# Local attention's maxima in items of two heads and one bank, with a third bank for its scores and a third for its outputs

## The reference, cut to what matters

```python
SWA_WINDOW = 128; SWA_KV_HEADS = 4; SWA_GROUP = 4   # four heads share one key/value head

def _banded_gqa(q, k, v, window, sinks):            # per block of 128 queries
    s = jnp.einsum('bqgrd,bkgd->bgrqk', qblk, kb).astype(jnp.float32) * scale
    s = jnp.where(mask, s, NEG_INF)                 # own block and the one before it
    snk = jnp.broadcast_to(sinks...)
    pr = jax.nn.softmax(jnp.concatenate([s, snk], -1), axis=-1)[..., :-1]
    return jnp.einsum('bgrqk,bkgd->bqgrd', pr, vb)

o * jax.nn.silu(z)
```

## Time and profile before

| | us |
|---|---|
| median of 3 runs | 3054.64 (3053.04 to 3061.67) |
| the profiled execution | 3053.61 |
| its span, first to last instruction | 3051.8 |
| TensorE busy in the span | 2892.7 (95%) |
| VectorE, ScalarE, GpSimd busy | 1938.8, 1590.5, 1392.0 |
| local attention, from the first maxima's product to the last output product | 476.1 to 728.7 |

### The profile page before, as it was taken

One profiled execution on the slowest core, in us unless ns is written; L12 is line 12 of the kernel. 1 busy time (PEld: TensorE's weight loads), 2 busy tenths in 40 slices (PEclk: granted clock), 3 DMA queues, 4 the chain that ended last, 5 costly groups with the idle time before them and its releaser, 6 DMA issues. The chain is left out here.

```text
span 3051.8 us, 41224 instructions
## 1 busy us (share of the span) xinstructions
PE 2892.7 (95%) x13411; PEld 2328.4 (76%) x13411; DVE 1938.8 (64%) x3398; ACT 1590.5 (52%) x2808; POOL 1392.0 (46%) x1139
## 2 busy tenths in 40 slices
PE   8999996888999999999998799999999999899998
PEld 6888884566888788777877588888888878688776
DVE  4543315663578864555664588888888887357875
ACT  3111114666445544444544277777777777534643
POOL 0022104665232540001440388888888889423353
PEclk9999997999999999999999699999999999999999
DMA  5343437565997675455799634435335342498674
GB/s 165 84 136 125 117 118 242 179 203 172 308 277 239 201 247 183 159 177 167 251 328 380 148 73 102 103 73 116 91 78 127 73 92 87 157 301 270 212 243 145
DMA packets 284760, 530.13 MB, mean 174 GB/s; under 512 B 29200, under 2 KB 110992, under 8 KB 277392
## 3 DMA queue, kind: packets, MB, share of 16 engines
q1 hardware_dynamic: 218528, 391.22, 43.3%
q10 hardware_dynamic: 66032, 136.48, 14.7%
HBM read 346.85 MB, written 180.49 MB: 173 GB/s over the span
## 5 line engine op out<-in xcount | busy, mean ns | idle before, releaser
L2609 POOL TENSOR_TENSOR mla_pl<-mla_p,mla_ph 128x512 fp32r<-128x512 f32 (+3 forms) x640 | 702.9, 1121 | 144.4 <-ACT mla_p L2458 141.5
L1523 PE MATMUL end_bank<-end_xh,end_whi 128*128 128x512 f32 x1808 | 718.1, 397 | 44.3 <-DVE end_wlo L1754 17.0
L1525 PE MATMUL end_bank<-end_xh,end_wlo 128*128 128x512 f32 x1808 | 708.2, 392 | 0.0
L1524 PE MATMUL end_bank<-end_xl,end_whi 128*128 128x512 f32 x1808 | 707.6, 391 | 0.0
L1592 ACT CAST end_whi<-early_wraw 128x1024 fp32r<-128x1024 f32 (+1 forms) x204 | 211.4, 1036 | 531.8 <-PE end_bank L1525 510.7
L2457 ACT ACTIVATE mla_ph<-mla_score 128x512 fp32r<-128x512 f32 (+3 forms) x640 | 342.4, 535 | 238.0 <-PE mla_score L2285 232.9
L1754 DVE TENSOR_TENSOR end_wlo<-early_wraw,end_whi 128x1024 fp32r<-128x1024 f32 x188 | 255.4, 1358 | 317.9 <-ACT end_whi L1592 317.7
L1523 PEld LDWEIGHTS end_bank<-end_xh,end_whi 128*128 128x128 f32 x1808 | 342.1, 189 | 134.9 <-DVE end_wlo L1754 24.6
L2542 DVE TENSOR_TENSOR mla_acc<-mla_acc,mla_p 128x512 f32<-128x512 f32 (+3 forms) x576 | 351.0, 609 | 106.6 <-ACT mla_p L2458 104.2
L1524 PEld LDWEIGHTS end_bank<-end_xl,end_whi 128*128 128x128 f32 x1808 | 342.3, 189 | 72.6 <-issue 2.9
L1525 PEld LDWEIGHTS end_bank<-end_xh,end_wlo 128*128 128x128 f32 x1808 | 341.6, 189 | 72.4
(11 more groups left out here) (242 smaller groups left out, 4985.7 us busy)
## 6 DMA issues: line engine op xcount, KB each, us to landing
early_wraw<-in_pe_gate ACTq DMA_DIRECT2D x64, 512.0 KB, 4.9
early_wraw<-in_w_out ACTq DMA_DIRECT2D x62, 512.0 KB, 7.3
early_wraw<-in_w_in ACTq DMA_DIRECT2D x56, 512.0 KB, 3.8
scratch_q<-in_rope SPq DMA_DIRECT2D x64, 256.0 KB, 2.9
swa_q<-scratch_q SPq DMA_DIRECT2D x8, 2048.0 KB, 9.2
end_factor<-scratch_inv SPq DMA_DIRECT2D x64, 256.0 KB, 9.6
scratch_proj<-end_out_f SPq DMA_DIRECT2D x64, 256.0 KB, 6.9
scratch_sum<-end_out_f SPq DMA_DIRECT2D x64, 256.0 KB, 6.3
```

The costliest lines, as they stand in the source:

```text
L1523: nc.tensor.matmul(bank, wh[:, at], xh[:, k0 + k * nq, :], start=(k == 0), stop=False)
L1524: nc.tensor.matmul(bank, wh[:, at], xl[:, k0 + k * nq, :], start=False, stop=False)
L1525: last = nc.tensor.matmul(bank, wl[:, at], xh[:, k0 + k * nq, :], start=False, stop=(k == kc - 1))
L2609: pool.tensor_tensor(p_lo[b][:, off:TC], prob[b][:, off:TC], p_hi[b][:, off:TC].bitcast(F32), ALU.subtract).then_inc(p_lo_ok, 1)
```

## The change

The item of the maxima is cut in two: two heads, 512 columns, one bank. The two `mx` tiles shrink from two banks to one each. The two banks that this frees go to a third score bank (`nscore` 3) and a third output bank (`n_o` 3). A unit has 16 items instead of 8; `share` puts them at 2, 2, 1, 2, 2, 2, 1, 2, 2 in slots 0 to 8 of an even unit and 3, 1, 2, 2, 1, 2, 2, 1, 2 in those of an odd one. An item still waits for the item two before it. The number of products and of DVE instructions is the same, and the maxima land in the same columns. `mla` keeps its banks; only the way its output column is written in the code changes.

```diff
-        lag, nbuf, nscore = (3, 6, 3) if long else (2, 5, 2)
+        lag, nbuf, n_o = (3, 6, 2) if long else (2, 5, 3)
+        nscore = 3
...
-        o_ps = [s.ps(f"o{b}", [P, TC]) for b in range(2)]
+        o_ps = [s.ps(f"o{b}", [P, TC]) for b in range(n_o)]
...
                 pe.wait_ge(probs, g + 1)
-                if st["first"] and c >= 2:
-                    pe.wait_ge(row_ok, c - 1)
+                if st["first"] and c >= n_o:
+                    pe.wait_ge(row_ok, c - n_o + 1)
                     if not long:
-                        pe.wait_ge(gated, c - 1)
+                        pe.wait_ge(gated, c - n_o + 1)
...
-                out = mx[:].rearrange("p (j n) -> p j n", j=x["groups"])[:, :, x["col"]:x["col"] + 1]
+                out = [mx[:, col:col + 1] for col in range(x["col"], n_mx, x["per"])[0:x["groups"]]]
...
             width = P * len(blks)
-            it.append(dict(products=[(j * half_b * P + c * P, blks[0][0] * P, width, "window_q", j * 2 * P)
-                                     for j in range(GROUP)],
-                           stride=2 * P, groups=GROUP, width=width, col=c))
+            for j0 in range(0, GROUP, 2):
+                it.append(dict(products=[((j0 + j) * half_b * P + c * P, blks[0][0] * P, width, "window_q", j * 2 * P)
+                                         for j in range(2)],
+                               stride=2 * P, groups=2, width=width, col=j0 * half_b + c, per=half_b))
...
-                max_cols=half_b * GROUP, max_width=2 * TC, items_to=8, long=False,
+                max_cols=half_b * GROUP, max_width=TC, items_to=8, long=False,
```

More of the change, by code:

```diff
@@ L2339, in weigh @@
                 pe.wait_ge(probs, g + 1)
-                if st["first"] and c >= 2:
-                    pe.wait_ge(row_ok, c - 1)
+                if st["first"] and c >= n_o:
+                    pe.wait_ge(row_ok, c - n_o + 1)
                     if not long:
-                        pe.wait_ge(gated, c - 1)
+                        pe.wait_ge(gated, c - n_o + 1)
                 v = vals[u % 2][:, st["v"], 0:P]
-                out, high, low = o_ps[c % 2][:, off:TC], p_hi[g % nbuf][:, off:TC], p_lo[g % nbuf][:, off:TC]
+                out, high, low = o_ps[c % n_o][:, off:TC], p_hi[g % nbuf][:, off:TC], p_lo[g % nbuf][:, off:TC]
                 mm(out, v, high, st["first"], False)
@@ L2355, in denominator @@
                 for j in range(TC // P):
-                    last = mm(o_ps[c % 2][:, j:j + 1], acc[c % 2][:, j * P:(j + 1) * P], consts["ones"][:, 0:1], True, True)
+                    last = mm(o_ps[c % n_o][:, j:j + 1], acc[c % 2][:, j * P:(j + 1) * P], consts["ones"][:, 0:1], True, True)
                 last.then_inc(den_ok, 1)
@@ L2405, in low_half @@
                     act.wait_ge(sum_ok, c - 1)
-                act.copy(o_low[c % 2][:], o_ps[c % 2][HEAD_DIM:P, :]).then_inc(low_ok, 1)
+                act.copy(o_low[c % 2][:], o_ps[c % n_o][HEAD_DIM:P, :]).then_inc(low_ok, 1)
             def denominators(c):
@@ L2411, in denominators @@
                     per = TC // P
-                    act.copy(den_cols[:, per * c:per * (c + 1)], o_ps[c % 2][:, 0:per]).then_inc(row_ok, 1)
+                    act.copy(den_cols[:, per * c:per * (c + 1)], o_ps[c % n_o][:, 0:per]).then_inc(row_ok, 1)
                     return
@@ L2416, in denominators @@
                     act.wait_ge(den_stored[c % small], 16 * (c // small))
-                act.copy(den_row[c % small][:], o_ps[c % 2][HEAD_DIM:HEAD_DIM + 1, :]).then_inc(row_ok, 1)
+                act.copy(den_row[c % small][:], o_ps[c % n_o][HEAD_DIM:HEAD_DIM + 1, :]).then_inc(row_ok, 1)
             def store_denominators():
@@ L2482, in item @@
                 src = mx_ps[n % len(mx_ps)][:].rearrange("p (j k) -> p j k", k=x["stride"])[:, 0:x["groups"], 0:x["width"]]
[L2483 removed]
+                out = [mx[:, col:col + 1] for col in range(x["col"], n_mx, x["per"])[0:x["groups"]]]
                 mask = x["products"][0][3]
                 if mask is None:
[L2486 removed]
+                    op = vec.tensor_reduce(out[0], src, AX.X, ALU.max)
                 else:
@@ L2491, in item @@
                                                       mt[:, mt.shape[1] - x["width"]:mt.shape[1]], 1.0, LOWEST,
-                                                      ALU.add, ALU.max, out[:, j, :])
+                                                      ALU.add, ALU.max, out[j])
                 op.then_inc(mx_done, 1)
@@ L2563, in out_gate @@
                     dve.wait_ge(stored[c % small], 16 * (c // small))
-                vec.tensor_tensor(o_out[c % small][:], o_ps[c % 2][0:HEAD_DIM, :], gate[c % n_gate][:], ALU.mult
+                vec.tensor_tensor(o_out[c % small][:], o_ps[c % n_o][0:HEAD_DIM, :], gate[c % n_gate][:], ALU.mult
                                   ).then_inc(gated, 1)
@@ L2699, in mla_config @@
                 items.append(dict(products=[(i * P, kc * TC, width, mask, 0)], stride=TC, groups=1,
-                                  width=width, col=len(items)))
+                                  width=width, col=len(items), per=1))
     def load(u, q_tile, k_tile, part):
```

2 lines of the change are left out of this document (1 added, 1 removed).

## The result

| | before | changed |
|---|---|---|
| median, runs on one chip | 3053.86 us (3053.04 to 3061.67) | 3082.16 us (3078.86 to 3085.53) |
| ratio, 95% interval | | 1.0087 [1.0067, 1.0107], or +20 to +33 us |
| the profiled execution, its span | 3053.61, 3051.8 | 3085.53, 3083.7 |
| VectorE, ScalarE, GpSimd busy | 1938.8, 1590.5, 1392.0 | 1940.5, 1590.8, 1394.4 |
| local attention, first maxima's product to last output product | 252.6 us | 276.4 us |

Slower, as forecast, but by 28 us instead of 10. The busy times of the three other engines moved by less than 3 us, so no work was added. In the profiled execution 23.9 us of the difference lie in the phase that was edited. What follows it took 2323.2 us before and 2329.2 after, but that part moves between 2319.5 and 2331.0 in all the profiled executions of this study, whatever was edited, so the phase's length is read from here on.

A forecast was written before the change was run, and what follows sets the result against it. TensorE nearly bound the kernel, but VectorE was longer in slots 0 to 8. Terms +11.9, -2.4 and +0.9 summed to +10.4 us, forecasting 3065.0 us; likeliest case 3059 to 3073, full range 3044 to 3072.

The forecast's parts named there:

- VectorE's nine slots: Slots 0 to 8 of a local-attention unit: VectorE's 17.1 us of work against TensorE's 16.4, so VectorE sets the pace.
- Rival A: Output and score bank waits vanish and nothing replaces them: 3032 us, or 3039 if stores still hold ScalarE; chance 0.14.
- signs of being right: Maxima's waits over 20 us, gate's under 2, landing waits 13 to 20, a unit's largest gap at slot 6 behind the copy.
- The rule from the copy: Last pair of maxima (slot 8) starts 7.3 us after the start of VectorE's query copy in odd units, 7.05 in even.
- the one on the third score bank: Unit boundaries: gain of 0.4 us, counted only in units 0 and 6; elsewhere a ScalarE store, unmoved, sets the pace.
- rival B: Lateness repaid at boundaries: loads start about 1.2 us earlier, out of the stores' way; -6.4 us, 3058.6, chance 0.20.
- gain of 0.4 at units 0 and 6: Third score bank's boundary gain of 0.4 us, counting only in the two units where no store is waited for.
- I booked 2.4: Third output bank: saves the slot 10 wait after the last item in units 1, 3 and 5, 0.8 us each.
- The lead-in: Unit 0's own items before the loop: VectorE idles 0.1 us per item, less 0.46 for an earlier start; +0.9 us.
- Unit 0: Its last pair of maxima (slot 8) starts at 509.6 instead of 508.8 us: +0.8 us.
- Unit 5: Its last pair of maxima starts at 664.6 instead of 661.8 us, with a copy 1.1 us longer: +2.8 us.
- Rival C: Gaps of some 3.5 us in units 3 and 5 might halve TensorE's clock, costing 8 us: 3073 us, chance 0.08.

The follow-up runs named there:

- the second execution: A second profiled execution of the unaltered changed kernel, the fastest of its chip: 3073.5 us (its runs' median 3081.8), local attention 272.5 us.

## Why the prediction was right or wrong

**The direction was right, and the mechanism in the main.** VectorE's nine slots and the landings ahead of them are the chain, the gate's waits are taken over by the maxima's (1.8 to 32.0 us, "over 20" was said), the swa_o waits for the gate are gone, and those for GpSimd's low parts grew from 1.8 us in 4 to 3.2 in 6. Rival A, faster by 15 to 22 us, asked for maxima's waits under 8; they are 32. But two of the signs of being right failed: the waits for landings are 28.0 us and not 13 to 20, and a unit's largest gap stands behind the copy only in units 3 and 6; in units 1, 2, 4 and 5 it stands ahead of it, behind a landing (2.26, 4.65, 4.96 and 2.76 us).

**The rule from the copy held.** The last items' products after, to be read beside the earlier trace rows:

```profile
583.86 0.77 PE L2286 MATMUL swa_mx<-swa_k,swa_q 128*128 128x256 f32 x4
...
619.00 0.65 PE L2286 MATMUL swa_mx<-swa_k,swa_q 128*128 128x256 f32 x4
```

These are two pairs each, the last starting 0.235 later: 584.1 in unit 2, where copy + 7.05 is 583.8, and 619.2 in unit 3, where copy + 7.3 is 616.8. Units 1, 2, 4 and 5 are within 0.35 us. Units 0 and 6 come 0.5 and 1.1 us later, and there the copy itself took 2.63 and 3.25 us instead of some 2.3. In unit 3 the missing 2.4 us are mostly the lower clock behind a gap of 3.58: in the run that kept TensorE busy the last pair started 8.1 us behind the copy instead of 9.7, with a copy that took 0.5 longer. What missed is when the copy starts. From the gathering before it to the copy it was 5.7 and 5.8 us longer than before in units 2 and 4, where my terms make it 0.7.

**The step that failed** is the one on the third score bank: "the next unit's pace is set by a store issued by ScalarE at this boundary (below), whose time this doesn't move". The time of its issue isn't moved, that of its landing is, since the loads gain 1.5 us on it: 12.8 us instead of 9.0 in unit 2. I saw that the loads would start earlier, and wrote it into rival B with the sign reversed ("may be out of the stores' way"). They do not come out of the way, because the store of chunk 5 follows the load before and after; more of the load is ahead of it. That is the term mis-sized in units 2 and 4, 4.2 and 4.1 us against 0.25 each; put at 0 in the sum, it measured 5.2 to 6.9 us for the two together when the bank alone was added to the halved items. At the boundaries into units 1, 3 and 5 the load's lead did not move (4.07 us now, 3.86 before into unit 1, to chunk 5's issue), and of the 1.7 us too many in unit 1 none can be put on the bank: unit 1's first gate waited 1.69 us for a landing of 11.0 us, in the second execution the same period was 1.8 us shorter.

The sum without that step can be compared with a kernel: the change with two score banks has no gain of 0.4 at units 0 and 6, and the prediction's 0.4 for them went into none of the terms that it added up, so those stay at 10.4; its phase grew by 11.4 and its time by 12.5 us [8, 17]. The agreement is partly luck: the halved items alone cost 18.0 us of phase where my terms give 12.8, and the third output bank gave back 6.6 where I booked 2.4. Unit 3 has the greatest share of both: 5.9 us against 3.2 in the first, and 4.3 of the second, with a landing that moved by 2.4 us for no reason that a run shows. The rest of the second, 2.3 us, is what I had booked for the bank.

**Smaller terms.** The lead-in: 1.5 for 0.9; at the lower clock two pairs take 1.76 us there where one item of four heads took 1.53. Unit 0: 1.8 for 0.8, its first pairs being at the lower clock until 502.1 (496.7 before). Unit 5: 1.5 for 2.8; its copy took 2.27 us this time and not the 3.38 of the earlier trace rows, and I had carried that 1.1 over (why it varies stands in the last section). The last unit: 0.6 for 0.

**Rival C** was right that the lower clock comes. It said units 3 and 5; it came in units 1 to 4, and in the second execution in 2 to 5. Its price of 8 us was too high: keeping TensorE busy gave 0 to 3 us. I had charged each slow slot in full, although VectorE was the later of the two in them.

**The range** ended at 3072, built on the forecast's and rival C's bounds. Neither held a landing that moves the wrong way: the store was the thing on which the middle units' pace rested, and its landing was given no bound on the slower side.

**The rule of the Trainium skill** (Perfetto Trace Analysis, § Optimization Strategy) takes the regular gap as a possible sign of too little SBUF or PSUM for the next tile; the prediction took up only PSUM. On PSUM the trace agrees in small part: the third output bank gave 6.6 us of phase, 5 by ratio, where it was tried with two score banks, and nothing with three. On SBUF it agrees: six output tiles took the gate's waits from 13.7 to 2.8 us and 13.5 us off the phase, with the eight banks as they were.

## What to carry to other kernels

Ask of a regular wait what stands behind its releaser, and whether that is an engine or a transfer; a buffer on the wrong side of it only moves the wait. When an edit lets an engine run ahead, list every transfer that is started by its progress and the small ones that then travel beside them, and give both signs a price. When a buffer is cut finer, keep its depth in work, not in pieces: two tiles of half an item cost 17 us by ratio, four tiles of half an item nothing that could be measured. Half-height tiles packed in pairs were the cheapest depth here.

## What the runs showed of the hardware

A store's landing grows by more than the lead of a large load over it, but the lead alone doesn't set it. At the boundaries into units 2 and 4, over all profiled runs with three output tiles, chunk 5's store of 128 KB landed 8.2 to 10.1 us after its issue where the load led by 2.95 us (twelve times), and 11.6 to 14.3 where it led by 4.2 to 4.5 (ten times), by the landings themselves; the gates that waited for them started some 0.1 later. At the boundaries into units 1, 3 and 5, leads of 3.8 to 4.4 us gave 9.2 to 11.6 (27 times; three runs in which the lead was another there are left out). What goes with the extra 3 us in units 2 and 4 is one more store in the load's shadow on the same queue: chunk 4's landed 1.8 us after its issue in all of the twelve, and after 7.0 to 9.3 us in all of the ten. But at the other boundaries it is behind the load as well, so no run here separates the two.

While both queues had work, they sent about the same number of packets, whatever their size: 537 and 560 in 563 to 572 us of the changed kernel, with 2.55 and 0.37 MB. Behind the loads the small packets came through at 407 per us.

TensorE fell to the lower of its two clocks in or right behind its gaps of 3.6 to 5.0 us and stayed there for 6.8 us in the records; in the second execution it was 3.4 us behind two gaps of 4.3 and 3.6, and 6.8 behind gaps of 4.2 and 2.6. In the changed kernel with six output tiles there are six gaps of 1.96 to 2.00 us: those in units 1, 3 and 5 ended in 3.4 us of it (from 538.5, 600.0 and 661.4), those in units 2, 4 and 6 did not. In this phase it cost next to nothing, as the engine was waiting for another.

VectorE's copy of the queries took 2.27 to 3.40 us with the same shape, and the traces show what goes with it. In 77 of the 144 copies of the 18 profiled executions no instruction of GpSimd ran when the copy started, or for at most 0.1 us more, and the copy took 2.27 or 2.28. In the other 67 it took 2.14 to 2.15 us plus what was left of GpSimd's instruction. The copy at 656.59 in the earlier trace rows, 3.38 long, is one of these; the instruction that ran then, and the one behind it:

```profile
656.54 1.28 POOL L2609 TENSOR_TENSOR swa_pl<-swa_p,swa_ph 128x512 fp32r<-128x512 f32 x1 [0.42 <-ACT swa_p L2458]
658.43 2.66 POOL L2609 TENSOR_TENSOR swa_pl<-swa_p,swa_ph 128x512 fp32r<-128x512 f32 x1 [0.61 <-ACT swa_p L2458]
```

1.23 us of the first were left, and 2.15 + 1.23 = 3.38. The second started inside the copy and took 2.66 instead of 1.28: it ended 1.12 us behind the copy, and all 126 such instructions of GpSimd ended 1.12 to 1.16 us behind it. So it looks as if each held the other up, whichever came first. No run was made to test this; it is read from the traces alone.
